# Twenty rows of the expert lookup moved into the picking stage, and one-hot tiles made by ScalarE in a decoder-step kernel

## Chip, cores and metric

The kernel runs on 1 core of a Trainium2 chip. The metric is the device time of one execution in microseconds (us), the median of several runs. Engines are named as in the profile: PE is TensorE, DVE is VectorE, ACT is ScalarE, POOL is GpSimd, SP is SyncE (which here only issues transfers).

## The reference, cut to what matters

One step of a hybrid autoregressive decoder: 512 prompt tokens and 8 sample tokens of 2048 features in float32 go through gated linear attention, a spatial gating unit and cross-attention, and then through PEER, a lookup of single-neuron experts. Only PEER and the final norm are touched:

```python
q = (hf @ w_q).reshape(N, 8, 2, 128)
s1, s2 = ...                              # scores against 128 + 128 sub-keys
# top 16 of each, then top 16 of the 256 sums: 8 heads * 16 = 128 experts per token
idx = e1 * 128 + e2
gate = softmax(sv)
a = einsum('nhkd,nd->nhk', u_tab[idx], h)     # one dot product per expert
coef = gate * gelu(a)
out = einsum('nhk,nhkd->nd', coef, v_tab[idx])
```

Both tables have 128 x 128 = 16384 rows of 2048 floats (8 KB).

## The kernel before

The tokens are worked in two groups. Group A holds the first two tiles of 128 prompt tokens and the 8 sample tokens; group B holds the last two tiles of 128 (y = 0 and y = 1). The two groups look their experts up in different ways.

**Group A: rows.** POOL gathers by indirect DMA. What the code calls a row is one such gather: 128 table rows of 8 KB, 1 MB in all, one for each token of the tile, into one of six buffers (`RING = 6`). DVE uses a row either in a dot product with the tokens (`dot`, L2968, from table u) or by adding it, weighted, to the result `acc` (`accumulate`, L2973, from table v). There are 128 u rows and 128 v rows for each of the two tiles, numbered 0 to 511, then 8 u rows (512 to 519) and 8 v rows (520 to 527) for the sample tokens. POOL may gather row g when DVE has used row g - 6. Between the sample's u and v rows ACT takes a gelu (L3175), and after tile 1's last v row POOL stores `acc` to memory (L2914), 1 MB, before it gathers the sample's v rows. DVE's program reaches the rows through a generator: `beside(k, limit)` does the next k of them, up to the limit, amid DVE's other work. `gone` counts the calls; call m works on row m - 2 (the first call only prepares). With 528 rows the last call is number `N_ROWS` = 529, and it also closes the tile.

**Group B, table stage** (`dve_table`, `act_table`, `pe_table`, `sp_table`; `NU = 128`). For group B the dot products are not gathered: PE multiplies all of table u, streamed from memory in 128 blocks of 1 MB into four buffers, with the 256 tokens of group B (L3132, 32 matmul instructions for a block). ACT copies each block's result for tile 0 to `a_tile` (L3089) and for tile 1 to `a_stage` (L3090), from where SP stores it. PE may run at most three blocks ahead of ACT. Beside it DVE takes the top 16 of 8 heads for each of B's tiles (`top_head`) and calls `beside` once in each turn of its own loop of 128. This loop does not wait for blocks. It is tied to ACT's turns only by softmaxes and gelus: DVE waits for ACT's exp of the sample tokens (`act_soft(act, S_T)`, L2836) before it uses row 476. The limit `U_ROWS` holds rows back for later: with 520, row 518 is the last one used in the table stage.

**Group B, picking stage** (`dve_last`, `act_last`, `pe_last`, `sp_last`). The needed 128 of 16384 products of each token are picked out in 32 groups of four slots. For each group PE spreads the second half of the index (`pe_hot`, L3341), a one-hot tile is made from it in SBUF (`make_hot`, L3239, one DVE instruction on 128x512), PE multiplies it with `a_tile` (`pe_select`, L3356), and DVE picks with four instructions (`pick`, L3248). PE's order is the select of group g, then the hot of group g + 2. The PSUM tiles of both are double, so PE can be two groups ahead of `pick`; there are four one-hot tiles. This is done for y = 0 in a stage of its own, and for y = 1 later, between the rows of y = 0.

**Group B, rows** (`gather_b`, L2947). The 128 v rows of each tile are gathered into seven buffers; three of four are added up by DVE (L3275), every fourth by PE (L3374). The first of them waits until DVE has used all 528 rows of group A (`row_used` at `V_Y[0]` = 528). SP's queue has, in this order: the load of the final gains and others when the table stage is over, the load of `a_tile` for y = 1 (8 MB, L3151, after the last select of y = 0), and reloads of `acc` after the sample's result has been folded by PE (L3387).

Of the kernel before, what the change touches and what calls it, by code (L numbers as in the profile page):

```python
# [9 lines left out]
ACT = mybir.ActivationFunctionType  # L10
# [27 lines left out]
NU = NK  # L38
GROUP = 4
GROUPS = P // GROUP  # L40
# [88 lines left out]
def mixer_kernel(nc, ins, outs):  # L129
    ctx = ExitStack()  # L130
    with ctx:
# [15 lines left out]
        iota_p = sb("iota_p", [P, 1], F32, 2560)  # L147
# [181 lines left out]
        dots_s = sb("dots_s", [P, TS], F32, R_SM + 2720)  # L329
        gelus_s = sb("gelus_s", [P, TS], F32, R_SM + 2752)  # L330
# [14 lines left out]
        oh = sb("oh", [P, 4, GROUP, SLOTS], F32, R_M)  # L345
# [7 lines left out]
        psum = ctx.enter_context(nc.psum_tensor("psum", [P, 8, 512], F32))  # L353
# [138 lines left out]
        dots_ready = sem("dots_ready")  # L492
        gelu_ready = sem("gelu_ready")
# [3 lines left out]
        hot_turned = sem("hot_turned")  # L497
# [3 lines left out]
        oh_ready = sem("oh_ready")  # L501
# [2249 lines left out]
        N_DOTS = 4  # L2751
        N_ROWS = V_S + TS + 1
        SOFT = (0, 1, 4, 2, 3)
        U_ROWS = V_S
        TURN_E1 = (50, 84)

        def top_head(dve, t, k):
# [324 lines left out]
        def act_table(act):  # L3082
            for i in range(NU):
                act.wait_ge(out_ready, OUTS_U + i + 1)
                if i >= 4:
                    act.wait_ge(z_stored[i % 4], 16 * z_stores_u(i))
                if i == 80:
                    act.wait_ge(ef_ready, 1)
                nc.scalar.activation(a_tile[:, i, :], bank_b(OUTS_U + i)[:, 0:P], ACT.Copy)  # L3089
                nc.scalar.activation(a_stage[:, i % 4, :], bank_b(OUTS_U + i)[:, P:WB], ACT.Copy).then_inc(evac_done, 1)  # L3090
                for y in range(2):
                    if i == TURN_E1[y]:
                        act.wait_ge(pturned, y + 1)
                        nc.scalar.activation(e1t[y][:], psum[:, 4 + y, 0:P], ACT.Copy).then_inc(e1_ready, 1)
                if i == 10:
                    act_soft(act, 1)
                if i == 30:
                    act_gelu(act, 2)
                if i == 44:
                    act_soft(act, 3)  # L3100
                if i == 64:
                    act_gelu(act, 3)
                if i == 76:
                    act_soft(act, 4)
                if i == 101:
                    act_soft(act, S_T)

        def dve_table(dve, beside):
            for i in range(NU):
                for y, i0 in enumerate((3, 35)):  # L3110
                    k = (i - i0) // 4
                    if (i - i0) % 4 == 0 and 0 <= k < PH:
                        if k == 0:
                            dve.wait_ge(sc_ready_b, 2 + y)
                        top_head(dve, 3 + y, k)
                        if k == PH - 1:
                            dve.drain().then_inc(sc_used, 1)
                            dve.drain().then_inc(idx_ready, 1)
                            dve.drain().then_inc(ef_ready, 1)
                    if i == i0 + 30:  # L3120
                        soft_first(dve, 3 + y)
                    if i == i0 + 46:
                        soft_second(dve, 3 + y)
                beside(1 if i % 6 == 0 else 2, U_ROWS)

        def pe_table(pe):
            pe.wait_ge(sc_ready_b, 3)
# [43 lines left out]
            sp.dma_start(outs["y_prompt"][t * P:(t + 1) * P, :], src[:]).then_inc(y_stored, 16)  # L3171

        def act_last(act):
            act.wait_ge(dots_ready, N_DOTS + 1)
            nc.scalar.activation(gelus_s[:], dots_s[:], ACT.Gelu).then_inc(gelu_ready, 1)  # L3175
            act_gelu_b(act, 0)
            for d in range(2):
                act_diags(act, 0, d)
            act.wait_ge(norm_loaded, 16)
            act_norm(act, 0, acc, P)  # L3180
            act.wait_ge(norm_loaded, 32)
            act_norm(act, 1, acc, P)
            act_diags(act, 0, 2)
            act.wait_ge(acc_ready, 4)
            act_norm(act, 2, htok2, TS)
            act_diags(act, 0, 3)
            act_gelu_b(act, 1)
            for d in range(2):
                act_diags(act, 1, d)
            act.wait_ge(acc_ready, 5)  # L3190
            act_norm(act, 3, acc_b[0], P)
            for d in range(2, 4):
                act_diags(act, 1, d)
            act.wait_ge(acc_ready, 6)
            act_norm(act, 4, acc_b[1], P)

        def act_diags(act, y, d):

# [14 lines left out]
        def act_norm(act, q, x, rows):  # L3213

            nc.scalar.activation(squares[0:rows, :], x[0:rows, :], ACT.Square,
                                 accum_out=small[0:rows, 0:1]).then_inc(squares_ready, 1)
            act.wait_ge(root_in, ROOTS_Y + q + 1)
            nc.scalar.activation(small[0:rows, 2:3], small[0:rows, 1:2], ACT.Sqrt).then_inc(root_out, 1)
# [33 lines left out]
                dve.drain().then_inc(a_picked, 1)  # L3252

        def select(dve, y, g):
            if g == 0:
                make_hot(dve, y, 0)
            if g + 1 < GROUPS:
                make_hot(dve, y, g + 1)
            pick(dve, y, g)

# [25 lines left out]
        def dve_last(dve, beside):  # L3286
            dve.wait_ge(e1_ready, 2)
            for g in range(GROUPS):
                select(dve, 0, g)
                if g % 4 == 3:  # L3290
                    beside(1)
            beside(N_ROWS)
            turn_a(dve, 0)
            dve.wait_ge(gfin_loaded, 48)
            weigh_b(dve, 0)
            dve.wait_ge(folded, 1)
            nc.vector.tensor_tensor(htok2[:].rearrange("p (b f) -> p b f", b=4), psum[0:TS, 0:4, :],
                                    htok2[:].rearrange("p (b f) -> p b f", b=4), ALU.add)
            tile_done(dve)
            for n in range(SLOTS):  # L3300
                if not on_pe(n):
                    accumulate_b(dve, 0, n)
                if n == 18:
                    norm_first(dve, 0, P)
                if n == 22:
                    norm_second(dve, 0, acc, P)
                if n == 44:
                    norm_first(dve, 1, P)
                if n == 48:
                    norm_second(dve, 1, acc, P)  # L3310
                if n == 54:
                    norm_first(dve, 2, TS)
                if n == 58:
                    norm_second(dve, 2, htok2, TS)
                if n >= 12 and n % 3 == 0 and (n - 12) // 3 < GROUPS:
                    select(dve, 1, (n - 12) // 3)
                if n == 112:
                    turn_a(dve, 1)
            weigh_b(dve, 1)
            dve.wait_ge(x1_loaded, 48)  # L3320
            for n in range(SLOTS):
                if not on_pe(n):
                    accumulate_b(dve, 1, n)
                if n == 2:
                    add_pe(dve, 0)
                if n == 8:
                    norm_first(dve, 3, P)
                if n == 12:
                    norm_second(dve, 3, acc_b[0], P)
            add_pe(dve, 1)  # L3330
            norm_first(dve, 4, P)
            norm_second(dve, 4, acc_b[1], P)
# [127 lines left out]
        @block.vector  # L3460
        def _(dve):
            dve_phase0(dve)
            dve_project(dve)
            dve_gla(dve)
            dve_merge(dve, N_BA, N_BC, True, beside=lambda: state_update(dve, 2, 8))
            dve_attention(dve, GA)
            dve_merge(dve, N_BC, N_BB, False)
            dve_spatial(dve, GA)
            dve_merge(dve, N_BB, N_OUT, False)
            dve_out(dve)  # L3470

            rows = experts_a(dve)
            gone = [0]

            def beside(k, limit=N_ROWS):
                for _ in range(min(k, limit - gone[0])):
                    gone[0] += 1
                    next(rows, None)

            dve_project_b(dve, beside)  # L3480
            dve_merge_b(dve, N_BA, N_BC, beside, (2,))
            dve_attention(dve, GB, beside)
            dve_merge_b(dve, N_BC, N_BB, beside, (2, 1))
            dve_spatial(dve, GB, beside)
            dve_merge_b(dve, N_BB, N_OUT, beside, (2, 1))
            dve.drain().then_inc(merged_ready, 1)
            dve_out_b(dve, beside)
            assert 270 < gone[0] < 300, gone
            dve_table(dve, beside)
            assert 500 < gone[0] <= U_ROWS, gone  # L3490
            dve_last(dve, beside)

# [110 lines left out]
```

## Time and profile before

| | us |
|---|---|
| median of 3 runs | 4749.39 (4745.84 to 4749.94) |
| the profiled execution | 4750.96 |
| its span in the trace | 4749.2 |
| PE busy | 4138.9 (87%) |
| DVE busy | 3131.6 (66%) |
| ACT busy | 868.2 (18%) |
| POOL busy | 1318.4 (28%) |

Times inside the trace are from the start of the span. The table stage starts at about 3004 us and ends at about 3951; picking for y = 0 goes to about 4043; the rows of group B go to the end at 4749.

### The profile page before, as it was taken

What the parts mean: (1) busy time and instruction counts of PE and PEld (TensorE: products, weight loads), DVE (VectorE), ACT (ScalarE), POOL (GpSimd) and SP (SyncE); (2) the same over time, 40 slices, a digit from 0 to 9 for tenths busy, and PEclk for the clock granted to TensorE, in tenths of its full rate; (3) what the DMA queues carried; (4) which work ended last, traced back from release to release, by engine and by line L of the source; (5) the groups of instructions that cost most, each with busy time, mean ns of one, the idle gap of its engine ahead of it and who ended that gap; (6) DMA issues with size and microseconds to landing.
All of it is one profiled execution on the core that took longest, in us unless ns stands there. A gap on an engine that the chain in (4) does not pass through costs nothing.

```text
span 4749.2 us, 62014 instructions
## 1 busy us (share of the span) xinstructions
PE 4138.9 (87%) x23876; PEld 3599.6 (76%) x23876; DVE 3131.6 (66%) x4575; ACT 868.2 (18%) x1257; POOL 1318.4 (28%) x822
## 2 busy tenths in 40 slices
PE   7999999999899999999775798999999999577555
PEld 7999999999788997887665576887788778344122
DVE  7434234443746647867679876788898656698776
ACT  4334334423332342011000000000000000000000
POOL 0000000000000003333444534344444330476665
PEclk9999999999898999999887798999999999788777
DMA  5555467875354549997999899999999993999998
GB/s 218 192 207 191 146 232 290 292 281 179 103 220 173 212 160 383 414 383 294 418 395 374 321 423 412 422 423 423 423 401 424 423 403 143 391 406 393 421 422 363
DMA packets 304986, 1519.48 MB, mean 320 GB/s; under 512 B 36586, under 2 KB 111802, under 8 KB 138212
## 3 DMA queue, kind: packets, MB, share of 16 engines
q0 software_dynamic: 114288, 830.54, 42.4%
q1 hardware_dynamic: 190500, 686.34, 38.2%
q8 instruction: 120, 1.97, 0.2%
q14 instruction: 78, 0.64, 0.0%
HBM read 1439.05 MB, written 77.71 MB: 319 GB/s over the span
## 4 chain that ended last, share of the span: by engine, by line
PE 50%; DMA 26%; DVE 10%; issue 6%; DVEq 3%; POOL 3%; ACT 2%; ACTq 0%; SPq 0%; POOLq 0%
PE psum L551 28%; DMA sb_raw<-in_wstream 12%; PE psum L3132 10%; DMA sb_ring<-in_peer_v,sb_idx_all 9%; PE psum L605 5%; DMA sb_ring<-in_peer_u,sb_idx_all 4%; POOL sb_ring L2947 2%; PE psum L3374 2%; DVE sb_acc L2973 2%; DVE sb_ring L2968 2%; DVEq L2279 1%; DVE sb_acc_b L3275 1%; DVE sb_split L535 1%; PE psum L3356 1%; ACT sb_split L531 1%
## 5 line engine op out<-in xcount | busy, mean ns | idle before, releaser
L551 PE MATMUL psum<-sb_actr,sb_split 128*128 128x264 f32 x8112 | 1010.6, 286 | 31.6 <-DVE sb_actr L2451 12.2
L551 PEld LDWEIGHTS psum<-sb_actr,sb_split 128*128 128x128 f32 x8112 | 998.9, 190 | 36.9 <-issue 22.2
L535 DVE TENSOR_TENSOR sb_split<-sb_raw,sb_split 128x2048 fp32r<-128x2048 f32 x201 | 460.7, 2293 | 706.6 <-ACT sb_split L531 705.5
L2858 POOL DMA_INDIRECT sb_ring<-in_peer_u,sb_idx_all x256 | 408.9, 1597 | 1203.9 <-DVEq L3001 571.8
L2968 DVE CUSTOM_DVE_ANT_0 sb_ring<-sb_ring,sb_htok 128x2048 f32<-128x2048 f32 x264 | 597.4, 2291 | 175.9 <-DMA sb_ring<-in_peer_u,sb_idx_all 161.1
L2973 DVE SCALAR_TENSOR_TENSOR sb_acc<-sb_ring,sb_coef,sb_acc 128x2048 f32<-128x2048 f32 x256 | 601.8, 2351 | 142.3 <-DMA sb_ring<-in_peer_v,sb_idx_all 127.8
L2858 POOL DMA_INDIRECT sb_ring<-in_peer_v,sb_idx_all x256 | 433.8, 1694 | 608.8 <-DVE sb_acc L2973 522.9
L3374 PE MATMUL psum<-sb_ring,sb_diag 128*128 128x512 f32 x512 | 341.4, 828 | 242.9 <-DMA sb_ring<-in_peer_v,sb_idx_all 235.9
L3275 DVE SCALAR_TENSOR_TENSOR sb_acc_b<-sb_ring,sb_coef_b,sb_acc_b 128x2048 f32<-128x2048 f32 x192 | 451.4, 2351 | 129.3 <-DMA sb_ring<-in_peer_v,sb_idx_all 115.4
L2947 POOL DMA_INDIRECT sb_ring<-in_peer_v,sb_idx_all x256 | 435.1, 1700 | 296.7 <-DVE sb_acc_b L3275 129.7
L3132 PE MATMUL psum<-sb_h2b,sb_raw_u 128*128 128x256 f32 x2048 | 456.9, 382 | 22.2 <-DMA sb_raw_u<-in_wstream 20.1
L3132 PE MATMUL psum<-sb_h2b,sb_raw 128*128 128x256 f32 x2048 | 454.8, 381 | 17.8 <-DMA sb_raw<-in_wstream 17.7
L3374 PEld LDWEIGHTS psum<-sb_ring,sb_diag 128*128 128x128 f32 x512 | 131.3, 269 | 437.4 <-DMA sb_ring<-in_peer_v,sb_idx_all 269.3
L3132 PEld LDWEIGHTS psum<-sb_h2b,sb_raw_u 128*128 128x128 f32 x2048 | 386.7, 190 | 90.4 <-DMA sb_raw_u<-in_wstream 37.0
L3132 PEld LDWEIGHTS psum<-sb_h2b,sb_raw 128*128 128x128 f32 x2048 | 385.8, 190 | 85.0 <-DMA sb_raw<-in_wstream 34.2
L605 PE MATMUL psum<-sb_hxb,sb_raw 128*128 128x256 f32 x1824 | 409.2, 387 | 16.5 <-DMA sb_raw<-in_wstream 14.6
L531 ACT ACTIVATE sb_split<-sb_raw 128x2048 fp32r<-128x2048 f32 x201 | 384.5, 1913 | 210.3 <-PE psum L551 181.0
L605 PEld LDWEIGHTS psum<-sb_hxb,sb_raw 128*128 128x128 f32 x1824 | 353.3, 195 | 69.0 <-DMA sb_raw<-in_wstream 15.8
L551 PE MATMUL psum<-sb_actb_hi,sb_split 128*128 128x256 f32 x2048 | 369.0, 279 | 0.0
L551 PEld LDWEIGHTS psum<-sb_actb_hi,sb_split 128*128 128x128 f32 x2048 | 316.3, 188 | 0.0
L551 PE MATMUL psum<-sb_actb_lo,sb_split 128*128 128x256 f32 x1024 | 285.9, 279 | 0.0
L1327 POOL TENSOR_TENSOR sb_kd<-sb_bcum_a 128x1024 f32<-128x1024 f32 x1 | 1.9, 1897 | 730.0 <-DVE sb_att_s L866 730.0
(436 smaller groups left out, 4117.6 us busy)
## 6 DMA issues: line engine op xcount, KB each, us to landing
sb_raw<-in_wstream SPq DMA_DIRECT2D x386, 1024.0 KB, 7.2
sb_raw_u<-in_wstream SPq DMA_DIRECT2D x64, 1024.0 KB, 23.0
sb_states<-in_state SPq DMA_DIRECT2D x32, 512.0 KB, 3.6
sb_states_t<-in_stateT SPq DMA_DIRECT2D x32, 512.0 KB, 4.1
out_gla_s<-sb_states SPq DMA_DIRECT2D x32, 512.0 KB, 3.1
dram_z<-sb_zst SPq DMA_DIRECT2D x121, 132.0 KB, 3.2
dram_z_b<-sb_zst SPq DMA_DIRECT2D x77, 128.0 KB, 1.8
sb_vrow<-dram_v SPq DMA_DIRECT2D x8, 1024.0 KB, 5.2
```

What stands on the lines that cost most here:

```text
L531: nc.scalar.activation(split[:, slot, 0, :], raw[:, slot, :], ACT.Copy).then_inc(hi_ready, 1)
L535: nc.vector.tensor_tensor(split[:, slot, 1, :], raw[:, slot, :], split[:, slot, 0, :], ALU.subtract).then_inc(lo_ready, 1)
L551: last = nc.tensor.matmul(psum[:, bank, 0:ntok], w[a], acts(b, kt), start=(i == 0 and a == 0 and b == 0), stop=(i == len(kts) - 1 and a == 1))
L605: last = nc.tensor.matmul(bank_b(q), raw[:, k % 3, w0 + i * P:w0 + (i + 1) * P], acts[:, kt, 0:WB], start=(i == 0), stop=(i == len(kts) - 1))
L2279: dve.drain()
L2858: nc.gpsimd.indirect_dma_start(ring[g % RING][:], None, ins[table], bass.IndirectOffsetOnAxis(ap=col, axis=0)) \
L2947: nc.gpsimd.indirect_dma_start(ring_b[slot_b(y, n)][:], None, ins["peer_v"], bass.IndirectOffsetOnAxis(ap=idx_all[:, 3 + y, n:n + 1], axis ...
L2968: nc.vector.tensor_tensor_reduce(u[:], u[:], htok[:], 1.0, 0.0, ALU.mult, ALU.add, out).then_inc(row_used, 1)
L2973: nc.vector.scalar_tensor_tensor(out=a[:], in0=v[:], scalar=c, in1=a[:], op0=ALU.mult, op1=ALU.add).then_inc(row_used, 1)
L3132: last = nc.tensor.matmul(bank_b(OUTS_U + i), raw_u[u_slot(i)][:, kt * P:(kt + 1) * P], h2b[:, kt, :], start=(kt == 0), stop=(kt == KT - 1))
L3275: nc.vector.scalar_tensor_tensor(out=acc_b[y][:], in0=v[:], scalar=coef_b[y][:, n:n + 1], in1=acc_b[y][:], op0=ALU.mult, op1=ALU.add).then ...
L3374: last = nc.tensor.matmul(psum[:, b, :], diag[:, n // PE_EACH % DIAGS, :], v[:, b * 512:(b + 1) * 512], start=(n < PE_EACH), stop=(n >= SL ...
```

## The change

`U_ROWS` goes from 520 to `N_ROWS - 20` = 509, so row 507 is the last one used in the table stage and rows 508 to 527 (and the store of `acc` that follows row 511) come in the picking stage, one after each of the groups g with g % 8 in 0, 1, 3, 4 and 6. In the table stage the number of rows in a turn becomes an even division in place of two, two, two, two, two, one. Three of ACT's turns in the table stage are later (gelu 3 from block 64 to 68, the sample's exp from 101 to 108). The one-hot tiles of y = 0 are made by ACT, with two instructions each: |p - x| and then relu(1 - that).

```diff
-        U_ROWS = V_S
+        U_ROWS = N_ROWS - 20
...
-                if i == 64:
+                if i == 68:
                     act_gelu(act, 3)
...
-                if i == 101:
+                if i == 108:
                     act_soft(act, S_T)
...
-                beside(1 if i % 6 == 0 else 2, U_ROWS)
+                beside((U_ROWS - gone) * (i + 1) // NU - (U_ROWS - gone) * i // NU)
...
         def act_last(act):
-            act.wait_ge(dots_ready, N_DOTS + 1)
-            nc.scalar.activation(gelus_s[:], dots_s[:], ACT.Gelu).then_inc(gelu_ready, 1)
+            for g in range(GROUPS):
+                act_hot(act, g)
+                if g == 19:
+                    act.wait_ge(dots_ready, N_DOTS + 1)
+                    nc.scalar.activation(gelus_s[:], dots_s[:], ACT.Gelu).then_inc(gelu_ready, 1)
...
+        def act_hot(act, g):
+
+            act.wait_ge(hot_turned, g + 1)
+            if g >= 4:
+                act.wait_ge(sub_done, g - 3)
+            at = oh[:, g % 4].rearrange("p n s -> p (n s)")
+            nc.scalar.activation(at, psum[:, 6 + g % 2, :], ACT.Abs, bias=iota_p[:], scale=-1.0)
+            act.drain()
+            nc.scalar.activation(at, at, ACT.Relu, bias=1.0, scale=-1.0).then_inc(oh_ready, 1)
...
         def select(dve, y, g):
-            if g == 0:
+
+            if y == 1 and g == 0:
                 make_hot(dve, y, 0)
-            if g + 1 < GROUPS:
+            if y == 1 and g + 1 < GROUPS:
                 make_hot(dve, y, g + 1)
             pick(dve, y, g)
...
-                if g % 4 == 3:
+                if g % 8 in (0, 1, 3, 4, 6):
                     beside(1)
```

## Rows read from the trace of the kernel before

**Rows 1.** Windows: us, busy of each engine (instructions), PE clock, DMA share, GB/s.

```profile
4020.00:4042.00 22.00, 20.70 (x121) 19.37 (x119) 18.34 (x73) 0.00 (x0) 0.00 (x0) 1.00 0.00 1
...
4049.00:4056.00 7.00, 5.41 (x8) 0.78 (x6) 1.84 (x2) 5.02 (x17) 5.24 (x6) 0.70 0.81 346
...
4200.00:4400.00 200.00, 146.06 (x455) 88.35 (x453) 173.28 (x243) 4.46 (x11) 141.58 (x76) 0.84 0.98 398
...
4600.00:4700.00 100.00, 58.52 (x80) 22.27 (x80) 70.97 (x32) 0.00 (x0) 66.13 (x41) 0.74 1.01 422
```

**Rows 2.** Timeline of ACT: copies of blocks 0, 16, 88, 108, 120.

```profile
3012.88 0.28 ACT L3089 ACTIVATE sb_a_tile<-psum 128x128 f32<-128x128 f32 x1 [8.95 <-PE psum L3132]
3123.38 0.28 ACT L3089 ACTIVATE sb_a_tile<-psum 128x128 f32<-128x128 f32 x1 [6.46 <-PE psum L3132]
...
3651.92 0.28 ACT L3089 ACTIVATE sb_a_tile<-psum 128x128 f32<-128x128 f32 x1 [6.86 <-PE psum L3132]
...
3803.80 0.28 ACT L3089 ACTIVATE sb_a_tile<-psum 128x128 f32<-128x128 f32 x1 [6.72 <-PE psum L3132]
...
3896.52 0.28 ACT L3089 ACTIVATE sb_a_tile<-psum 128x128 f32<-128x128 f32 x1 [7.12 <-PE psum L3132]
```

**Rows 3.** DMA queues, 3700 to 3800: packets, MB, share.

```profile
q0 software_dynamic: 3823, 27.38, 65.1%
q1 hardware_dynamic: 3827, 14.92, 36.3%
```

**Rows 4.** Timeline of DVE about 3753 and at the table stage's end.

```profile
3752.60 0.28 DVE L2826 TENSOR_REDUCE sb_sums<-sb_gate_all 128x8 f32<-128x128 f32 x1
...
3757.90 2.35 DVE L2973 SCALAR_TENSOR_TENSOR sb_acc<-sb_ring,sb_coef,sb_acc 128x2048 f32<-128x2048 f32 x1 [1.67 <-DMA sb_ring<-in_peer_v,sb_idx_all]
...
3765.46 2.35 DVE L2973 SCALAR_TENSOR_TENSOR sb_acc<-sb_ring,sb_coef,sb_acc 128x2048 f32<-128x2048 f32 x1 [1.66 <-DMA sb_ring<-in_peer_v,sb_idx_all]
...
3952.26 1.57 DVE L3239 TENSOR_SCALAR sb_oh<-psum,sb_iota_p 128x512 f32<-128x512 f32 x2 [24.72 <-PE psum L3341]
```

**Rows 5.** Timeline of picking: a group with a row, then a plain one.

```profile
3985.78 0.36 DVE L3248 SCALAR_TENSOR_TENSOR psum<-sb_iota_n,sb_e1t,psum 128x128 f32<-128x128 f32 x1 [0.81 <-PE psum L3356]
...
3986.86 2.35 DVE L2973 SCALAR_TENSOR_TENSOR sb_acc<-sb_ring,sb_coef_s,sb_acc 128x2048 f32<-128x2048 f32 x1
...
3989.12 0.75 DVE L3239 TENSOR_SCALAR sb_oh<-psum,sb_iota_p 128x512 f32<-128x512 f32 x1
...
3989.92 1.60 PEld L3356 LDWEIGHTS psum<-sb_a_tile,sb_oh 128*128 128x128 f32 x8 [0.84 <-DVE sb_oh L3239]
...
3992.55 1.62 PEld L3356 LDWEIGHTS psum<-sb_a_tile,sb_oh 128*128 128x128 f32 x8
...
3994.18 1.09 PEld L3341 LDWEIGHTS psum<-sb_ef,sb_ident 128*128 128x128 f32 x8
...
3995.19 1.62 PEld L3356 LDWEIGHTS psum<-sb_a_tile,sb_oh 128*128 128x128 f32 x8
```

**Rows 6.** Timeline: start and end of picking, start of B's rows.

```profile
3951.02 2.02 PE L3341 MATMUL psum<-sb_ef,sb_ident 128*128 128x128 f32 x16 [0.63 <-ACT sb_a_stage L3090]
...
3953.06 1.59 PEld L3356 LDWEIGHTS psum<-sb_a_tile,sb_oh 128*128 128x128 f32 x8 [0.21 <-DVE sb_oh L3239]
...
4042.26 0.32 SPq L3151 DMA_DIRECT2D sb_a_tile<-dram_a  x1
...
4043.64 4.81 DVE L2973 SCALAR_TENSOR_TENSOR sb_acc<-sb_ring,sb_coef_s,sb_acc 128x2048 f32<-128x2048 f32 x2 [0.21 <-issue]
...
4049.24 0.94 POOL L2947 DMA_INDIRECT sb_ring<-in_peer_v,sb_idx_all  x1 [58.29 <-DVE sb_acc L2973]
```

**Rows 7.** Groups of ACT by shape: mean ns is the second number.

```profile
L725 ACT ACTIVATE sb_states<-sb_states,sb_es_cur 128x512 f32<-128x512 f32 x64 | 42.8, 718 | 3.1 <-issue 0.4
...
L2091 ACT ACTIVATE sb_probt<-psum 128x512 f32<-128x512 f32 x8 | 4.8, 600 | 3.4 <-PE psum L2050 3.4
...
L2836 ACT ACT_TABLE_LOAD x4 | 5.1, 1283 | 0.1
```

More of the change, by code:

```diff
@@ L3104, in act_table, with dve_table @@
                     act_soft(act, 4)
-                if i == 101:
+                if i == 108:
                     act_soft(act, S_T)
-        def dve_table(dve, beside):
+        def dve_table(dve, beside, gone):
             for i in range(NU):
@@ L3488, in _ @@
             assert 270 < gone[0] < 300, gone
-            dve_table(dve, beside)
+            dve_table(dve, beside, gone[0])
             assert 500 < gone[0] <= U_ROWS, gone
```

## Prediction

> **What bounds the kernel now.** I read the page's busy shares in 40 slices first. From the table stage on the DMA row is all but full, except in the slice that holds picking. I then cut that part into windows, and went into timelines of single engines for the stages that the change touches.
>
> In the table stage (3004 to 3951) the two queues move 27.38 + 14.92 MB in 100 us of one stretch, 423 GB/s [rows 3]. PE sets its end, but PE has two paces. Blocks 0 to 16 take (3123.38 - 3012.88) / 16 = 6.91 us each, which is PE's own pace; blocks 88 to 120 take (3896.52 - 3651.92) / 32 = 7.64 [rows 2]. In the second state DVE waits for rows and PE for blocks, and between them the queues divide the transfer engines: 3823 packets for rows against 3827 for the stream, one for one, but 27.38 MB against 14.92 [rows 3]. A row's packet is about twice as large, so two rows go by for one block. DVE shows it too: from 3757.90 to 3765.46, two rows in 7.56 us [rows 4]. So a hungry DVE slows a block by 7.56 - 6.91 = 0.65 us and gets two rows for it: **each MB that DVE or POOL takes in this state costs the stage 0.33 us**, not the 2.48 us that 1.05 MB takes at 423 GB/s. DVE has done its share of rows 24.72 us before the stage ends [rows 4].
>
> In picking (3951 to 4043) the transfer engines are nearly idle: 1 GB/s in its last 22 us [rows 1]. PE is the bound. In a plain group the select's loads start at 3992.55, the hot's at 3994.18 and the next select's at 3995.19, so a group is 1.63 + 1.01 = 2.64 us; DVE has slack, it waits 0.81 for a select [rows 5]. When a row comes between, DVE's 2.26 us (3986.86 to 3989.12) delay its next one-hot tile, and PE stands idle 0.84 [rows 5]. From the first select at 3953.06 to the load that follows the last at 4042.26 are 89.2 us [rows 6]; 30 x 2.64 and 3.7 for the last two selects make 82.9, so the seven groups with a row in between cost 0.9 each. After the last pick DVE still has two rows, 4.81 us, and only then can POOL gather for group B, at 4049.24 [rows 6].
>
> From 4042.26, when the 8 MB load of `a_tile` is issued, the transfer engines bound the rest: 346 GB/s in a short dip, later 398, at the end 422 [rows 1, 6]. DVE comes close between 4200 and 4400 (173 of 200 us busy), and the rate there is 6% below the limit.
>
> **The change part by part.**
>
> *Eleven rows leave the table stage.* Rows 508 to 518 were used there and now are not, and with a ring of six the fetched ones end eleven sooner too. The 1 MB store of `acc`, which follows row 511, also leaves. That is 12 MB x 0.33 = 3.9 us less. The bounds: nothing, if the blocks that gain were not waiting; 12 x 2.48 = 29.8 us, if the stage's time were its bytes.
>
> *The even spread.* DVE's loop does not wait for blocks, so one or two rows in a turn changes only how rows fall between the heads. I cost it at 0.
>
> *Later turns of ACT.* DVE comes to row 476 at 3752.60 [rows 4]; ACT's turn 108 is at 3803.80 [rows 2]. So DVE will now stand about 50 us for the sample's exp. Queued behind it are 32 rows (476 to 507), and POOL, whose ring is full. Six of the rows will have landed by then; the last 26 come at 3.78 us, 98 us. DVE ends at about 3804 + 6 + 98 = 3908, 39 us before the stage ends at 3947; I allow 15 of these for the sample's indices and tokens, which POOL fetches in between. The pause costs nothing as long as this cover is there; without it each further us of DVE would count in full. POOL's own order is unchanged.
>
> *One-hot tiles on ACT.* Per group DVE loses an instruction of 0.75 [rows 5] and ACT gains two instructions on 128x512. The nearest rows are 600 ns from PSUM and 718 in SBUF with a per-partition operand [rows 7]; the pair lies between 2 x 0.60 and 2 x 0.72 plus a drain that no row shows, which I bound by nothing and a full small instruction, 0.28. I take 1.45, range 1.2 to 1.7. It fits: from the end of PE's hot g + 2 to its select g + 2 lie the select g + 1 and the hot g + 3, 2.64 us. So PE no longer waits for anybody. At the start the first tile comes 1.45 - 0.75 = 0.7 later.
>
> The table of "Use VectorE, not ScalarE" for relu speaks against this move (the Trainium skill, "ScalarE: Activation LUTs", "Rules for kernel authors"). Per instruction the rows agree: 0.75 on DVE against two of at least 0.60. By that rule the stage would be 32 x 0.7 = 22 us longer if the tile's time were on the path; by the timeline, with PE the path, it is 0.7 once.
>
> *Twenty rows in picking.* DVE's work is 32 x 1.08 for the picks (3985.78 to 3986.86 [rows 5]) and at most 20 x 2.26 for the rows, 80 us, against PE's 32 x 2.64 = 84.5. The densest stretch is two rows in consecutive groups, 2 x (1.08 + 2.26) = 6.7 against 5.3, which being two groups ahead absorbs. At g = 17 DVE waits for the gelu of the sample, which ACT takes after its tile 19 with a table load (1.283 [rows 7]) that it can do ahead; DVE's slack holds it. The ring holds six landed rows at the start and the transfers run in idle time: 14 rows, the store and 2 MB of loads are some 18 MB, 45 us of 88.
>
> *Sum for picking.* Seven waits of PE go, 7 x 0.9 = 6.3, and 0.7 comes at the start: the load of `a_tile` is asked for **5.6 us sooner**, at 4036.7 by the old clock. Row 527 is used after g = 30, at about 4038.2, so POOL starts on B's rows at about 4039, 10 us sooner against 4049.24.
>
> *Group B.* It is bound by bytes, which stay the same, so the end moves with the start of the load: 5.6. Its dip to 346 GB/s, (423 - 346) x 7 / 423 = 1.3 us, may vanish since rows now are queued at once; between 0 and 1.3 I take 0.5.
>
> Sum: 3.9 + 5.6 + 0.5 = 10.0 us. From the profiled execution's 4750.96 that is 4741; the median of the runs is 1.6 lower, so **4739**.
>
> **The rivals.**
>
> *No gain to speak of.* The middle of group B is close to DVE's bound and PE's: it may give back what the earlier start brings, or lose by another phase of rows and selects. If half of picking's gain and none of the dip come through, and the table stage gives nothing because the pause moves its rows to blocks near the end, the sum is 2.8: 4746.5. For it: 398 GB/s between 4200 and 4400, 6% of 200 us = 12 us that nothing in my sum explains. Against: at 4600 to 4700 rows flow at 422, DVE waiting.
>
> *Bytes are all.* If the table stage's time is its bytes, the 12 MB give 29.8, with the 6.1 behind it 36: 4713. For it: 423 GB/s where I looked [rows 3]. Against: PE's 6.91 us a block is a floor, 128 x 6.91 = 884 of the stage's 947 us, and DVE's rows end before the stage does, so bytes taken away there leave the transfer engines idle.
>
> *Slower: ScalarE becomes picking's bound.* A group then takes ACT's pair. Above 2.64 us each 0.1 costs 3.2 us, and at 2.64 + 10 / 32 = 2.95 the whole gain is gone. If |x| and relu each brought a table load in every group, the pair would be 1.45 + 2 x 1.283 = 4.0 and picking 32 x (4.0 - 2.64) = 44 us longer: 4783. For it: a load does come at exp and gelu [rows 7]. Against: it comes four times in all, not at each copy between an exp and a gelu. The Trainium skill ("ScalarE: Activation LUTs", "Table sets: the hidden batching unit") says that abs, relu and copy are in every set, by which there would be no load but gelu's; no row here has Abs or Relu.
>
> **How the numbers follow.** Forecast, 7 to 15 us less: 0.55. No gain to speak of, from 7 less to 9 more: 0.29. Bytes are all, 15 less or more: 0.10. Slower: 0.06. No change that can be measured is within 0.2% here, 9.5 us. Of the forecast's 0.55 about three quarters lie beyond 9.5, so faster is 0.41 + 0.10 = 0.51, same 0.43, slower 0.06. The forecast's own range is 4734 to 4743. The range for 8 in 10 takes in the case without gain and the near part of the large one: 4727 to 4751.
>
> **What would show it.** The first picking instruction of PE at about 3947 in place of 3951.02; DVE standing some 50 us at L2826 and done with rows before the table stage ends; ACT pairs of about 1.45 us; PE without gaps, a select each 2.64 us; the load of `a_tile` at about 4033 and the first gather of B at about 4035; the same length from that load to the end. The prediction is wrong if blocks in the hungry state change pace (then my 0.33 per MB is wrong), if PE waits for ACT's tiles, or if the end of group B does not move with its start.

## The result, and the profile after

| | before | changed |
|---|---|---|
| median (5 runs each) | 4749.94 us (4745.84 to 4758.73) | 4726.17 us (4719.40 to 4730.37) |
| ratio, 95% interval | | 0.9945 (0.9931 to 0.9960) |
| span of the profiled execution | 4749.2 | 4717.3 |

The change makes the kernel 24 us faster, more than twice the 10 us forecast and just outside the range, whose lower end was 4727. (It moves two of ACT's turns in the table stage, gelu 3 and the sample's exp, and not three as the text ahead of the prediction says.) Four marks cut both traces into stages: ACT's copy of the first and of the last block of the table stage, the issue of the load of `a_tile`, and the end of the span.

| stage, us | before | changed | difference | forecast |
|---|---|---|---|---|
| up to the first copy | 3012.9 | 3009.7 | -3.2 | 0 |
| table stage, first to last copy | 937.5 | 918.1 | **-19.4** | -3.9 |
| last copy to the load of `a_tile` | 91.8 | 86.7 | -5.1 | -5.6 |
| from that load to the end | 706.9 | 702.7 | -4.2 | -0.5 |

Each stage is read from one profiled execution of a kernel. In the fourteen experiments below the first row lies between 3007.6 and 3017.8 and the last between 706.7 and 713.3, with nothing changed that bears on them, and the profiled execution of the changed kernel was the fastest of its five; so neither difference says much. In the table stage, blocks 16 to 64 take 363.3 us in the changed kernel and 365.5 to 366.1 in e1, e3, e5, e6 and e13, whose edits reach nothing before block 64: a difference of less than 3 us between the stages of two runs says nothing by itself. The other two make 24.5 us, which is near the difference of the medians, 23.8. Picking came out as predicted; the table stage gave five times what it should have.

Picking first. These are lines of the timeline of the changed kernel at the start and end of the stage (in its file L3133 is the table's matmul, L3356 the hot, L3371 the select, L3262 the pick, L3207 and L3209 are ACT's two instructions).

```profile
3928.46 2.02 PE L3356 MATMUL psum<-sb_ef,sb_ident 128*128 128x128 f32 x16 [0.63 <-ACT sb_a_stage L3090]
...
3929.62 0.69 ACT L3207 ACTIVATE sb_oh<-psum,sb_iota_p 128x512 f32<-128x512 f32 x1 [1.31 <-PE psum L3356]
3930.38 0.63 ACT L3209 ACTIVATE sb_oh<-sb_oh 128x512 f32<-128x512 f32 x1
...
3931.06 1.60 PEld L3371 LDWEIGHTS psum<-sb_a_tile,sb_oh 128*128 128x128 f32 x8 [0.77 <-ACT sb_oh L3209]
...
3933.68 1.61 PEld L3371 LDWEIGHTS psum<-sb_a_tile,sb_oh 128*128 128x128 f32 x8
...
3936.32 1.61 PEld L3371 LDWEIGHTS psum<-sb_a_tile,sb_oh 128*128 128x128 f32 x8
...
4014.59 0.32 SPq L3152 DMA_DIRECT2D sb_a_tile<-dram_a  x1
...
4016.64 0.94 POOL L2947 DMA_INDIRECT sb_ring<-in_peer_v,sb_idx_all  x1 [25.45 <-DVE sb_acc L2973]
```

The answer to [rows 5, 6]: the pair ends 1.39 us after it began (3929.62 to 3931.01), and selects start every 2.62 to 2.64 us although DVE adds a row after groups 0 and 1. From the load of `a_tile` to POOL's first gather for group B are now 2.0 us instead of 7.0, since no rows trail.

Now the table stage. The windows of the changed kernel about DVE's stand at row 476 (columns as in [rows 1]), and two lines of DVE's timeline:

```profile
3767.00:3800.00 33.00, 32.60 (x151) 28.38 (x150) 2.79 (x4) 2.43 (x11) 0.00 (x0) 1.00 0.64 237
3800.00:3830.00 30.00, 30.00 (x141) 26.41 (x140) 24.37 (x12) 1.78 (x8) 21.80 (x13) 1.00 0.89 366
3830.00:3928.00 98.00, 97.61 (x452) 85.26 (x450) 48.87 (x21) 6.38 (x29) 28.47 (x32) 1.00 1.02 400
```

```profile
3568.52 0.29 DVE L2826 TENSOR_REDUCE sb_sums<-sb_gate_all 128x8 f32<-128x128 f32 x1 [6.24 <-ACT sb_gate_all L2836]
...
3796.83 0.29 DVE L2826 TENSOR_REDUCE sb_sums<-sb_gate_all 128x8 f32<-128x128 f32 x1 [45.11 <-ACT sb_gate_all L2836]
...
3842.20 2.35 DVE L2973 SCALAR_TENSOR_TENSOR sb_acc<-sb_ring,sb_coef,sb_acc 128x2048 f32<-128x2048 f32 x1 [2.57 <-DMA sb_ring<-in_peer_v,sb_idx_all]
...
3849.78 2.35 DVE L2973 SCALAR_TENSOR_TENSOR sb_acc<-sb_ring,sb_coef,sb_acc 128x2048 f32<-128x2048 f32 x1 [2.58 <-DMA sb_ring<-in_peer_v,sb_idx_all]
```

DVE stood 45.11 us, as predicted (about 50), and over its last 30 us the transfers fell to 237 GB/s. After it DVE is as hungry as ever: two rows in 7.58 us (3842.20 to 3849.78). By my price PE should then need 7.56 us a block. It does not: it is busy 97.61 of 98 us, and of blocks 105 to 126 only the last takes longer than 6.91 us (7.39). The second stand, 6.24 us, I had not foreseen at all.

ACT's copies show the pace. The table gives the time of the blocks between two copies; at PE's pace of 6.906 us a block the columns would read 331.5, 165.7, 110.5 and 158.8.

| blocks | 16 to 64 | 64 to 88 | 88 to 104 | 104 to 127 | stage |
|---|---|---|---|---|---|
| before | 362.3 | 166.3 | 122.0 | 176.5 | 937.5 |
| changed | 363.3 | 168.4 | 116.0 | 160.0 | 918.1 |

So 16.5 us come from the blocks after the long stand and 6.0 from the blocks after the short one, against 3.1 lost before. (In the table, "16 to 64" is the time from the copy of block 16 to that of block 64.)

### The profile page after: what moved, and what is told of

It reads as the page before. It is cut to its first block, busy times and chain, and to the rows that moved or that the text cites. A ratio compares the mean times of both kernels' runs of the same rounds, so it can differ in the third digit from the quotient of the medians.

```text
span 4717.3 us, 62078 instructions
## 1 busy us (share of the span) xinstructions
PE 4134.8 (88%) x23876; PEld 3599.6 (76%) x23876; DVE 3107.3 (66%) x4543; ACT 910.3 (19%) x1321; POOL 1329.1 (28%) x822
## 4 chain that ended last, share of the span: by engine, by line
PE 53%; DMA 23%; DVE 11%; issue 5%; DVEq 3%; POOL 3%; ACT 2%; ACTq 0%; SPq 0%; POOLq 0%
PE psum L551 29%; PE psum L3133 12%; DMA sb_ring<-in_peer_v,sb_idx_all 9%; DMA sb_raw_u<-in_wstream 7%; PE psum L605 5%; DMA sb_ring<-in_peer_u,sb_idx_all 4%; DMA sb_raw<-in_wstream 2%; DVE sb_acc L2973 2%; POOL sb_ring L2947 2%; PE psum L3389 2%; DVE sb_ring L2968 2%; DVE sb_acc_b L3290 2%; PE psum L3371 1%; DVEq L2279 1%; DVE sb_split L535 1%
## 5 line engine op out<-in xcount | busy, mean ns | idle before, releaser
L2858 POOL DMA_INDIRECT sb_ring<-in_peer_v,sb_idx_all x256 | 443.1, 1731 | 632.1 <-DVE sb_acc L2973 541.2
L2947 POOL DMA_INDIRECT sb_ring<-in_peer_v,sb_idx_all x256 | 438.5, 1713 | 261.2 <-DVE sb_acc_b L3290 134.6
L3133 PE MATMUL psum<-sb_h2b,sb_raw_u 128*128 128x256 f32 x2048 | 452.9, 381 | 15.9 <-DMA sb_raw_u<-in_wstream 13.9
L3133 PE MATMUL psum<-sb_h2b,sb_raw 128*128 128x256 f32 x2048 | 452.3, 380 | 12.0 <-DMA sb_raw<-in_wstream 11.9
L3133 PEld LDWEIGHTS psum<-sb_h2b,sb_raw_u 128*128 128x128 f32 x2048 | 386.6, 190 | 79.0 <-DMA sb_raw_u<-in_wstream 25.5
L3133 PEld LDWEIGHTS psum<-sb_h2b,sb_raw 128*128 128x128 f32 x2048 | 386.9, 190 | 74.3 <-DMA sb_raw<-in_wstream 22.8
```

Source lines behind the costliest of these rows:

```text
L2858: nc.gpsimd.indirect_dma_start(ring[g % RING][:], None, ins[table], bass.IndirectOffsetOnAxis(ap=col, axis=0)) \
L2947: nc.gpsimd.indirect_dma_start(ring_b[slot_b(y, n)][:], None, ins["peer_v"], bass.IndirectOffsetOnAxis(ap=idx_all[:, 3 + y, n:n + 1], axis ...
L3133: last = nc.tensor.matmul(bank_b(OUTS_U + i), raw_u[u_slot(i)][:, kt * P:(kt + 1) * P], h2b[:, kt, :], start=(kt == 0), stop=(kt == KT - 1))
```

## The experiments

Theory P: a stand of DVE lets the stream of blocks, which gathers normally hold to one MB in three, fill its four buffers, and PE then lives on them. Theory B: the stage is bound by its bytes, and the 12 MB taken out are worth more than 0.33 us each. Each ratio is against runs of the kernel before on the same chip. The last three columns are from ACT's copies in the profiled run.

| run | ratio (95%) | 88 to 104 | 104 to 127 | stage | last copy to load |
|---|---|---|---|---|---|
| e1 turns back | 0.9962 (0.9948 to 0.9975) | 114.6 | 174.2 | 932.6 | 86.7 |
| e2 ACT's tiles alone | 0.9981 (0.9971 to 0.9992) | 122.0 | 176.0 | 940.5 | 86.2 |
| e3 tiles on DVE | 0.9983 (0.9972 to 0.9994) | 114.3 | 160.3 | 916.7 | 106.6 |
| e4 tied, i - 4 | 0.9919 (0.9901 to 0.9938) | 111.5 | 162.0 | 911.0 | 86.7 |
| e5 exp at 104 | 0.9943 (0.9929 to 0.9957) | 114.4 | 164.3 | 920.7 | 86.7 |
| e6 exp at 112 | 0.9975 (0.9963 to 0.9988) | 114.3 | 159.5 | 917.9 | 95.8 |
| e7 tied, turns back | 0.9936 (0.9921 to 0.9951) | 111.2 | 166.9 | 918.2 | 86.7 |
| e8 old quota | 0.9956 (0.9943 to 0.9970) | 121.5 | 159.7 | 922.3 | 86.7 |
| e9 rows alone | 0.9975 (0.9966 to 0.9985) | 122.0 | 172.5 | 935.1 | 86.7 |
| e10 spread alone | 1.0003 (0.9994 to 1.0011) | 122.0 | 177.2 | 940.3 | 91.8 |
| e11 late turns alone | 1.0017 (1.0008 to 1.0027) | 122.0 | 159.3 | 923.6 | 117.8 |
| e12 tied, i - 2 | 0.9908 (0.9892 to 0.9924) | 112.5 | 164.6 | 903.6 | 86.7 |
| e13 exp of B's tile at 72 | 0.9969 (0.9957 to 0.9982) | 120.7 | 160.2 | 931.6 | 86.7 |
| e14 tied, i - 1 | 0.9902 (0.9884 to 0.9921) | 111.9 | 164.9 | 898.7 | 86.7 |

**e1: the changed kernel with ACT's turns put back.**

```diff
-                if i == 68:
+                if i == 64:
                     act_gelu(act, 3)
...
-                if i == 108:
+                if i == 101:
                     act_soft(act, S_T)
```

> The changed kernel with ACT's turns put back (gelu 3 at block 64, the sample's exp at block 101), so that DVE hardly stands at row 476. Theory P (the pause: while DVE stands, the stream fills its four buffers, and the 24 blocks after it live on that and run at 6.91 us): the pause's part goes, blocks 104 to 127 take about 7.6 again, the table stage is 14 to 17 us longer than in the changed kernel, total 4740 to 4743. Theory B (bytes: the 12 MB taken out of the stage are worth 1 to 2 us each, whatever DVE's order): no difference to the changed kernel, 4726.

Measured: the stage is 14.5 us longer than in the changed kernel (932.6 against 918.1). Of these, 2.2 lie in blocks 16 to 64, before the edit; blocks 64 to 104 are 1.9 shorter, since the short stand is 10.8 us in this run in place of 6.2; blocks 104 to 127 are 14.2 longer. The ratio goes from 0.9945 to 0.9962, some 8 us, known to about 9 us by the two intervals. Theory P, as far as the stage goes; B is out, since the bytes are those of the changed kernel. The moved gelu has no part in it: DVE does not wait for it in either trace (L2984). These are PE's waits, in the changed kernel from 3797 to 3928 and in e1 from 3797 to 3947:

```profile
PE psum L3133 <- DMA sb_raw<-in_wstream: 0.2, 1, 0.2
```

```profile
PE psum L3133 <- DMA sb_raw_u<-in_wstream: 5.5, 7, 3.1
PE psum L3133 <- DMA sb_raw<-in_wstream: 2.7, 6, 0.9
```

Not all of the 14.2 us is pace. One block of e1, number 112, takes 11.9 us: at that time (3830 to 3841) all transfers together fall to 228 GB/s, most likely for POOL's loads of the sample's tokens, issued from 3817 on. The same block or the one before it takes 9.1 us before, 10.9 in e9 and 13.6 in e10. The changed kernel has the dip too (212 GB/s from 3859 to 3868), and its blocks stay at 6.9. So about 4 us of the 14.2 are a stall that the filled buffers cover, and about 10 the slow pace.

**e2 and e3: the two halves of picking.** e2 is the kernel before with `act_hot`; ACT takes the sample's gelu after its tile 5. e3 is the changed kernel with `make_hot` for y = 0 on DVE and without `act_hot`.

> The kernel before with the one-hot tiles of y = 0 made by ACT and nothing else (8 rows in picking as before, row 519 after group 3, so ACT takes the sample's gelu after its tile 5). PE no longer waits in seven groups, the first select comes 0.6 later: picking 5 to 6 us shorter, the two trailing rows stay. Theory P and B alike: 4744 to 4745, 0.1% faster than before. If PE's waits were not the path: 4750.

> The changed kernel with the one-hot tiles of y = 0 made by DVE again; the 20 rows stay in picking. DVE then has 1.08 + 0.66 per group and 2.26 per row, 32 x 1.74 + 44 = 100 us and some waits, against PE's 86: picking 14 to 25 us longer than in the changed kernel. Theory P and B alike: 4740 to 4751. If the transfers of the rows, and not DVE, filled picking: 4727.

e2: picking is 5.6 us shorter (91.8 to 86.2), as worked out. e3: 106.6 us, 20 longer than with ACT's tiles; its table stage is as short as the changed kernel's (916.7). DVE, with tiles and 20 rows, bounds the stage then, so ACT's tiles are the condition for the rows. One line of PE's waits during picking shows who holds it (total, times, longest):

```profile
PE psum L3368 <- DVE sb_oh L3250: 15.0, 17, 1.8
```

**e5 and e6: a shorter and a longer stand.** The exp of the sample tokens at block 104 and at 112.

```diff
-                if i == 108:
+                if i == 104:        # e6: 112
                     act_soft(act, S_T)
```

> The changed kernel with the sample's exp at block 104 in place of 108: DVE stands at row 476 for some 15 us in place of 45. Theory P with buffers (credit): for the first 21 us of a pause the six gathers already issued still take their share, so the stream never has the transfers alone and its four buffers do not fill; the table stage is 930 to 933 us (first to last copy), as with the turns put back, total 12 to 15 us over the changed kernel. Theory L (each us of pause is worth the same, 14.5 of stage for 45 of pause): 15 of 45 give 5, stage 927 to 928, total 9 to 10 over the changed kernel.

> The changed kernel with the sample's exp at block 112: DVE stands for some 70 us. Credit: four buffers are full after some 33 us of pause, so a longer one adds nothing to the stream's start, but the slow blocks after it are fewer; stage 915 to 918. The 32 rows behind the pause need 121 us and end 15 to 20 us after the last block, so picking starts late by that less the two groups that PE can be ahead: picking 100 to 105 us against 86.7, total 12 to 18 over the changed kernel. Theory L: stage 910.

| stand of DVE, us | 0 (e1) | 14.4 (e5) | 45.1 (changed) | 72.1 (e6) |
|---|---|---|---|---|
| blocks 104 to 127 | 174.2 | 164.3 | 160.0 | 159.5 |

The stand saturates, as buffers do: the first 14.4 us give 9.9, the next 31 give 4.3, the next 27 give 0.5, and 158.8 is PE's floor. The other runs fall in line: the six with a stand of 42 us or more there (changed, e3, e6, e8, e11, e13) take 159.3 to 160.3 us for these blocks, the five with none or 2.3 us at most (before, e1, e2, e9, e10) 172.5 to 177.2. In e5 one can watch the buffers run empty: blocks 105 to 116 take 6.9 us each, blocks 118 to 124 take 7.6 again.

Both forecasts for e5 were wrong, 930 to 933 and 927 to 928 for 920.7 measured: I expected nothing, or a third, from 14.4 us because six gathers were still under way. In total e5 can't be told from the changed kernel (0.9943 and 0.9945). The DMA queues show what happens instead. First e5 from 3780 to 3790, just after its stand (packets, MB, share); then the changed kernel from 3770 to 3780, during its stand, and from 3870 to 3920, well after it.

```profile
q1 hardware_dynamic: 655, 2.62, 63.5%
q0 software_dynamic: 211, 1.59, 37.8%
```

```profile
q1 hardware_dynamic: 877, 3.31, 85.5%
q0 software_dynamic: 9, 0.03, 0.8%
...
q0 software_dynamic: 1889, 13.79, 65.6%
q1 hardware_dynamic: 1881, 7.26, 35.6%
```

In a hungry stretch the packets are one for one [rows 3]. In e5 the gathers asked for before the stand had landed by 3780, and those asked for after it were few, so for 10 us the stream has three packets to one. In the changed kernel it has all of them for a while (3.31 MB in 10 us). Later the packets are one for one again, and the stream's queue moves 7.26 / 5 = 1.45 MB in 10 us. At PE's pace it would need (1.05 + 0.07) / 6.91 x 10 = 1.61, with the store of `a_stage` counted, which uses the same queue. PE does not slow down: the difference comes out of the buffers.

e6 pays for its length: DVE's rows end at 3942.2, after the last copy at 3929.9, and picking takes 95.8 us (I had expected 100 to 105). Its ratio is 0.9975.

**e8, e9, e10: rows and spread taken apart.** e8 is the changed kernel with the old quota; e9 also has the turns put back; e10 is the kernel before with the even spread alone.

```diff
-                beside((U_ROWS - gone) * (i + 1) // NU - (U_ROWS - gone) * i // NU)
+                beside(1 if i % 6 == 0 else 2, U_ROWS)       # e8, e9
```

> The changed kernel with the old quota in DVE's turns (two, two, two, two, two, one) up to the new limit of 509: the same rows and the same pause, only less evenly set between the heads and over by turn 122. Since DVE does not wait for blocks, theory P and B alike: no difference to the changed kernel within 3 us, stage 916 to 920. If the even spread is what helps (by its ratio between heads and rows): stage 921 or more.

> The changed kernel without its spread and without its later turns: old quota in DVE's turns, gelu 3 at block 64, the sample's exp at 101; the limit of 509, the 20 rows in picking and ACT's one-hot tiles stay. What the 11 rows and the store are worth in the table stage by themselves. By 0.33 us a MB: 3.9, stage 934 to 937 us against 938 to 941 without. If they are worth their bytes: stage 911. Total by the first: picking's 5 and 2 to 4 here, 0.998 of the kernel before.

> The kernel before with the even spread alone (the same 234 rows in the 128 turns, limit 520). If the spread is worth what the three runs with and without it suggest: blocks 88 to 104 take 114 to 117 us in place of 122, stage 931 to 934, total 5 to 8 under the kernel before. If what counts there was that only 223 rows were spread: 122 and no change. My prediction had 0.

e9: the stage is 935.1 against 937.5 (before) and 940.5 (e2, with the same table stage); the rows alone are worth 2.4 to 5.4 us, which holds the 3.9 but is hardly more than two executions differ by. e10: the spread by itself, with the limit of 520, is worth nothing. e8: with the limit of 509 the old quota costs 4.2 us of stage, blocks 88 to 104 going back from 116.0 to 121.5 (expected: no difference). So the spread counts only together with the rows, and for that the 6.24 us stand was the suspect: DVE waits there for the exp of B's second tile, which ACT takes at block 76. The traces place DVE's use of that exp before row 428 in the changed kernel, before row 435 in e10 and before row 440 with the old quota: the fewer rows ahead of it, the earlier DVE comes. (They also correct a count in my expectations: 293 calls are over when the stage begins, so the stage spreads 216 rows with the limit of 509 and 227 with 520, not 223 and 234.) Of before, e9 and e10 no trace shows this wait; of the changed kernel, e1 and e5 each does (6.2, 10.8 and 13.1 us), and so do e3 (12.8) and e6 (12.4).

**e13: that stand taken away.**

```diff
-                if i == 76:
+                if i == 72:
                     act_soft(act, 4)
```

> The changed kernel with the exp of B's second tile at ACT's turn 72 in place of 76, so that DVE, which comes to it near 3562 us, no longer stands there; everything else as changed. If the stand is what saved time in blocks 88 to 104: these take 121 to 122 us in place of 116, blocks 76 to 80 lose their 2.5, stage 3 to 4 longer than 918 (920 to 923). If the even spread itself saved it: 116 stays and the stage is 915 to 916.

Blocks 88 to 104 take 120.7 us and the stage 931.6, 13.5 longer than in the changed kernel. Of these, 2.5 lie in blocks 16 to 64, before the edit, and say nothing; the other 11.0 are three times what I expected, since blocks 64 to 88 lose 6.0 too (174.4 against 168.4). Block by block: in both kernels the slow pace, which ends near block 60, begins again at block 76. In e13 it goes on to block 101; in the changed kernel the stand (3562.3 to 3568.5) falls at its start, it ends after three blocks, and blocks 79 to 94 run at 6.9 us. DVE still waits for the sample's exp, now longer, but that adds nothing since the buffers are full:

```profile
DVE sb_sums L2826 <- ACT sb_gate_all L2836: 67.4, 1, 67.4
```

Without that stand the even spread gives a longer stage than the old quota (931.6 against e8's 922.3), where the slow pace begins only at block 89. It was the stand, an accident of the spread, that paid.

**e11: the late turns alone,** with the limit of 520.

> The kernel before with ACT's later turns alone (gelu 3 at 68, the sample's exp at 108) and its limit of 520: 43 rows stand behind the pause in place of 32. Theory P: blocks 104 to 127 take 160 us, stage 922 to 926, but DVE's rows need 6 + 37 x 3.78 + 15 = 161 us after the pause and end some 30 us after the last block, so picking begins late: nothing of the 15 us arrives, total 0 to 12 slower than before. This is the run that tells what the 11 rows are for. If the 11 rows are not needed for it: total 10 to 15 under the kernel before.

Blocks 104 to 127 take 159.3 us, the stage 923.6, and the kernel is 0.17% slower. DVE's 43 rows behind the stand end late; its first one-hot tile is made at 3963.45, 27 us after the last copy (3936.6), where before it was 2 us after:

```profile
3963.45 1.41 DVE L3239 TENSOR_SCALAR sb_oh<-psum,sb_iota_p 128x512 f32<-128x512 f32 x2
```

So the eleven rows are worth little themselves; they are what makes room for the stand.

**e4, e7, e12, e14: rows really tied to the blocks.** DVE's turn waits for a block, so rows go evenly over them.

```diff
         def dve_table(dve, beside, gone):
             for i in range(NU):
+                if i >= 4:
+                    dve.wait_ge(out_ready, OUTS_U + i - 3)    # e4, e7: block i - 4
...
+                if i >= 2:
+                    dve.wait_ge(out_ready, OUTS_U + i - 1)    # e12: block i - 2
...
+                if i >= 1:
+                    dve.wait_ge(out_ready, OUTS_U + i)        # e14: block i - 1
```

e7 also has ACT's turns put back as in e1.

> The changed kernel with one wait more: DVE's turn i in the table stage waits until PE has finished block i - 4, so that rows really are spread evenly over the blocks. Theory P: what slows blocks is a hungry DVE; held to 1.74 rows a block it takes 423 GB/s less 152 for the stream, and all 128 blocks run near 6.91 to 7.1: the stage is 905 to 915 us against 918, total 4713 to 4723. Theory B: the stage is bound by its bytes as it is now, so the same, 4726, or later if DVE falls behind in the turns with heads. Should the wait make DVE late for picking: over 4730.

> The kernel with DVE tied to the blocks (turn i waits for block i - 4) and ACT's turns put back (gelu 3 at 64, the sample's exp at 101), so the tie is the only thing that holds DVE. If holding rows to 1.74 a block is what counts, wherever it is done: stage 908 to 914 us, as with the tie and the late turn (911), total as there, about 4720 and 6 under the changed kernel. If the pause at row 476 is needed: stage 925 to 930, total 8 to 14 over the changed kernel.

> The changed kernel with DVE's turn i waiting for block i - 2 (in place of i - 4 as in the tied run): DVE is held two turns later, so the slow blocks between 16 and 56 get fewer rows. Stage 907 to 911 against 911, total 0 to 4 under the tied run's. If DVE then is late at the pause's end or for picking: total above the tied run's.

> The changed kernel with DVE's turn i waiting for block i - 1, one later than in e12. If still more holding pays: stage 900 to 903 us against 903.6, total 4705 to 4711 beside 4713. If DVE now ends its rows after the last block: picking over 87 us and the total 4715 or more.

All four beat the kernel before, and the later the block that DVE waits for, the shorter the stage: 911.0, 903.6, 898.7. All of that gain is in blocks 16 to 64 (359.2, 349.5, 345.6); from block 64 on the three take 441.4, 443.6 and 442.6. e7 tells that the tie does much by itself (918.2 without any late turn, against 932.6 in e1), but less than I had expected (908 to 914). In e14 the hold is spread over many short waits (DVE's waits from 3000 to 3940; L3135 is the table's matmul there):

```profile
DVE sb_acc L2973 <- PE psum L3135: 73.9, 26, 5.2
DVE sb_ring L2968 <- DMA sb_ring<-in_peer_u,sb_idx_all: 30.0, 21, 5.1
DVE sb_top_v L2765 <- PE psum L3135: 19.5, 8, 4.6
```

e14 has the lowest ratio of this study, 0.9902 (0.9884 to 0.9921) of the kernel before, though the interval of e12 overlaps it nearly whole. Of what still lies above PE's floor there (898.7 against 877.1), 14.1 us are in blocks 16 to 64 (345.6 against 331.5) and 6.1 in blocks 104 to 127 (164.9 against 158.8).

## Why the prediction was wrong

*The step that failed* is "Later turns of ACT": I saw the stand of DVE, priced it only as a possible loss, and gave it 0. It is the largest term: 14.2 us in the blocks behind it (e1 against changed). A second, shorter stand made by the even spread, which I costed at 0 too, gives 11.0 from block 64 on (e13 against changed), of which the spread itself takes back 8.2 (e13 against e8, the same blocks).

*Why it failed.* "Each MB that DVE or POOL takes in this state costs the stage 0.33 us" was read from stretches where the state had lasted long. The pace of the stream was right; that PE takes this pace at once was not, because four block buffers of 6.9 us each stand between them. The price holds for a hungry stretch that goes on, and e9 agrees with it for the eleven rows and the store. A stand of 14.4 us fills enough to carry PE over twelve of the next 23 blocks. The cover that I asked for was there, but smaller than worked out: DVE's last row ends at 3919.1, 9 us before the last copy and not 39, since the stage itself ended earlier.

*Picking* was right: 5.1 us for 5.6, the pair 1.39 for 1.45, the first select 2.6 us after PE's start (3928.46 to 3931.06) against 2.0 before, PE without gaps. ACT did not become the bound: PE waited 0.6 us for its tiles, once. The Trainium skill ("ScalarE: Activation LUTs", "Rules for kernel authors") says to use VectorE for relu. No run here has a relu on DVE. For the tile the rows agree, one instruction of 0.75 on DVE against 0.69 + 0.63 on ACT; but "per instruction", as the prediction has it, they do not, since each of ACT's two is the shorter. To follow the rule would have been wrong here: DVE's time was what the rows needed (e3, 20 us). The Trainium skill ("ScalarE: Activation LUTs", "Table sets: the hidden batching unit") says that relu and abs are in every set, and the trace agrees: picking has one table load, gelu's, beside 64 relu and abs instructions.

*Group B.* I took 0.5 for the dip. In the experiments the part from the load to the end is 707 to 713 us, before it was 706.9, so 0.5 can't be told, and the 4.2 of the profiled run is not to be put down to the change.

*The rivals.* "Bytes are all" forecast a gain beyond 15 us, and that is what came, but by another mechanism: e1 has the same bytes and not the gain. "No gain to speak of" named the pause as harmful; it is harmful once DVE's rows end after the last block (e6, e11). The range left the gain of the stand out, so its lower end of 4727 was 0.8 us too high.

That a stand of 6 us can be worth 11, more than it lasts, follows from the buffers by an estimate that no run tests: in 6.24 us gathers move 1.7 MB in the hungry state (27.38 MB in 100 us, [rows 3]); put off, they leave room for 1.5 blocks of 1.11 MB (with the store of `a_stage`), and each of these would otherwise have taken 7.56 us, 11.6 in all. The rows put off cost nothing later, because DVE only stands less at row 476 (45.1 us in place of 67.4).

What stays open: why DVE is hungry from block 76 with the even spread and only from block 89 with the old quota (e8); it was not tried. That e1's stage and total differ from the changed kernel's by 14.5 and 8 us is no contradiction: the total is known to some 9 us only, and the profiled execution was the slowest of its runs in e1 and the fastest in the changed kernel.

## What to carry to other kernels

Where two streams share the transfer engines and only one of them feeds the bound, look at the other's consumer: each time it runs ahead it takes bandwidth that the bound could have stored, so holding it back (a wait on the bound's progress, or a late turn of a third engine) can be worth more than removing its bytes (here 14.2 us in the blocks behind the stand, and 2.4 to 5.4 for 12 MB fewer). Price a starved stage with its buffers in: a short interruption of the rival stream pays for many blocks afterwards. And a stand needs room behind it; check what of the held engine's work must be done before the next stage.

## What was unexpected of the hardware

While both queues had work waiting, the transfer engines served them packet for packet, so the share in bytes was set by the packets' size, not by need (gathers 7.2 KB a packet, stream 3.9 KB over 3700 to 3800, [rows 3]; 1889 packets to 1881 in the changed kernel from 3870 to 3920). A stand of 14.4 us, shorter than the 23 us that six outstanding gathers take at one per 3.78 us, still gave the stream 655 packets to 211 about 5 to 15 us after it. The likely reason, not tested by itself, is that gathers asked for again come back one by one.
